# The last slab of a gated-linear-attention trunk finished in two parts of 256 tokens, with GpSimd scaling the first part of the result

## The reference, cut to what matters

```python
y = concat(y_h, y_g) @ w_out ;  h = h + y
e = rms_norm(p @ ple_proj, ple_norm_w)
gate = sigmoid(rms_norm(h, ple_gate_norm_w) @ ple_gate_w + ple_gate_b)
h = h + gate * e
return rms_norm(h, final_norm_w)          # row norm over all 2048 features
```

## Time and profile before

| what | us |
|---|---|
| median of three runs | 2304.66 |
| the profiled execution | 2304.73 |
| its span, first to last instruction | 2302.7 |

### The profile page before, as it was taken

How to read it: one execution, slowest core, us unless ns; L and a number is a source line. 1 busy time by engine, 2 the same in 40 slices (tenths; PEclk the granted TensorE clock), 3 DMA queues, 4 the chain that set the end, 5 groups by cost and what they waited for, 6 DMA issues and landing times.

```text
span 2302.7 us, 30712 instructions
## 1 busy us (share of the span) xinstructions
PE 2234.5 (97%) x10528; PEld 1855.6 (81%) x10528; DVE 1476.4 (64%) x2913; ACT 998.4 (43%) x1695; POOL 0.2 (0%) x4
## 2 busy tenths in 40 slices
PE   6999999999999999999999999999999999999995
PEld 5688888888888878888888888887888887787884
DVE  4667777775576567677766555566336456767776
ACT  5444455444343434444444333442224334446443
POOL 0000000000000000000000000000000000000000
PEclk9999999999999999999999999999999999999997
DMA  7522222222222224222222222223644543343452
GB/s 277 187 84 86 82 80 93 94 79 82 88 93 90 83 74 156 82 81 92 94 79 78 96 93 81 83 92 102 207 128 158 167 160 101 119 128 100 150 166 103
DMA packets 88501, 257.24 MB, mean 112 GB/s; under 512 B 9296, under 2 KB 9552, under 8 KB 88432
## 3 DMA queue, kind: packets, MB, share of 16 engines
q1 hardware_dynamic: 88432, 256.35, 33.7%
HBM read 231.15 MB, written 25.17 MB: 111 GB/s over the span
## 4 chain that ended last, share of the span: by engine, by line
PE 89%; DVE 4%; ACT 3%; DMA 2%; issue 1%; SPq 0%; DVEq 0%; ACTq 0%; POOLq 0%
PE acc L497 26%; PE acc L499 26%; PE acc L498 26%; PE lv L562 3%; PE so L551 1%; PE so L573 1%; PE so L571 1%; DMA e_scratch<-work 1%; DVE w_lo L1111 1%; DVE act_lo L1130 1%; DMA w_raw<-in_slabs 1%; ACT act_hi L770 1%; PE ms L540 1%; ACT w_hi L727 1%; PE tr L585 0%
## 5 line engine op out<-in xcount | busy, mean ns | idle before, releaser
L497 PE MATMUL acc<-act_hi,w_lo 128*128 128x512 f32 x2880 | 1158.2, 402 | 34.3 <-DMA vecs<-in_vec 12.2
L498 PE MATMUL acc<-act_lo,w_hi 128*128 128x512 f32 x2880 | 1126.8, 391 | 0.0
L499 PE MATMUL acc<-act_hi,w_hi 128*128 128x512 f32 x2880 | 1126.5, 391 | 0.0
L497 PEld LDWEIGHTS acc<-act_hi,w_lo 128*128 128x128 f32 x2880 | 544.6, 189 | 153.9 <-issue 16.0
L499 PEld LDWEIGHTS acc<-act_hi,w_hi 128*128 128x128 f32 x2880 | 543.2, 189 | 114.9
L498 PEld LDWEIGHTS acc<-act_lo,w_hi 128*128 128x128 f32 x2880 | 544.8, 189 | 104.2 <-issue 1.7
L727 ACT CAST w_hi<-w_raw 128x1024 fp32r<-128x1024 f32 x356 | 358.3, 1047 | 495.5 <-PE acc L499 444.5
L1111 DVE TENSOR_TENSOR w_lo<-w_raw,w_hi 128x1024 fp32r<-128x1024 f32 x356 | 419.7, 1219 | 80.1 <-ACT w_hi L727 79.9
L784 ACT ACTIVATE work<-work 128x512 f32<-128x512 f32 x120 | 75.7, 630 | 170.6 <-DVE work L1167 169.9
L741 ACT ACTIVATE work<-work 128x512 f32<-128x512 f32 x96 | 60.7, 633 | 129.3 <-DVE work L1147 129.3
L1181 DVE COPY_PREDICATED work<-mask_sb,lv 128x256 f32<-128x256 uint8 x168 | 88.7, 528 | 7.3
(11 more groups left out here) (212 smaller groups left out, 1808.5 us busy)
## 6 DMA issues: line engine op xcount, KB each, us to landing
w_raw<-in_slabs SPq DMA_DIRECT2D x356, 512.0 KB, 4.1
work<-e_scratch SPq DMA_DIRECT2D x64, 256.0 KB, 4.7
feat<-in_x_feat SPq DMA_DIRECT2D x8, 1024.0 KB, 11.1
e_scratch<-work SPq DMA_DIRECT2D x32, 256.0 KB, 2.2
state_h<-in_x_feat SPq DMA_DIRECT2D x32, 256.0 KB, 2.6
y_scratch<-work SPq DMA_DIRECT2D x16, 256.0 KB, 2.0
y_scratch<-work SPq DMA_DIRECT2D x8, 512.0 KB, 2.8
feat<-y_scratch SPq DMA_DIRECT2D x4, 1024.0 KB, 9.0
```

The source lines that it names most:

```text
L497: nc.tensor.matmul(ps, lhs_lo, rhs_hi, start=start, stop=False)
L498: nc.tensor.matmul(ps, lhs_hi, rhs_lo, start=False, stop=False)
L499: return nc.tensor.matmul(ps, lhs_hi, rhs_hi, start=False, stop=stop)
```

## The change

The last slab's 48 matmuls of 512 columns become twice 48 of 256 columns: first all for tokens 0 to 255 into `acc[1]`, then all for tokens 256 to 511 into `lv_ps[0]`. The gate chain of that tile is made once for each part, `last_first(0)`, `last_rest(0)`, `last_first(1)`, `last_rest(1)` on VectorE and two `g_gate` calls on ScalarE. The row sums, the variance, the inverse root and the four correcting instructions are made for each part too. When the first part's factor is done, `fr_ready` lets GpSimd scale all 16 tiles for tokens 0 to 255; VectorE scales the 16 tiles for tokens 256 to 511. SyncE stores each part with five DMAs of 4, 4, 4, 2 and 2 tiles: first the five of part 0 (waiting for GpSimd), then the five of part 1 (waiting for VectorE). The core of the diff:

```diff
+        PARTS = (slice(0, TH // 2), slice(TH // 2, TH))
-        ROWS_X, ROWS_H, ROWS_E, ROWS_F = (1, 2), (3, 6), (4, 5), (7, 8)
+        ROWS_X, ROWS_H, ROWS_E, ROWS_F = (1, 2), (3, 6), (4, 5), (7, 8, 9)
 @@ sync
-            for n in range(KT):
-                store_out(1, n)
-            sp.wait_ge(out_stored, HALVES * KT * 16)
+            STORES = (4, 4, 4, 2, 2)
+            for u in range(2):
+                n = 0
+                for count in STORES:
+                    n += count
+                    sp.wait_ge((f_part, f_scaled)[u], n + u * KT)
+                    sp.dma_start(out[1, n - count:n, :, PARTS[u]].rearrange("k p n -> p k n"),
+                                 work[:, n - count:n, PARTS[u]]).then_inc(out_stored, 16)
 @@ gpsimd
+            pool.wait_ge(fr_ready, 1)
+            for n in range(KT):
+                nc.gpsimd.tensor_tensor(work[:, n, PARTS[0]], work[:, n, PARTS[0]],
+                                        f_r[1][:, PARTS[0]], ALU.mult).then_inc(f_part, 1)
 @@ tensor
-            with pe.Fori(1, KT // 2) as i:
+            with pe.Fori(1, KT // 2 - 1) as i:
                 g_pair(1, i)
-            row_sums(ROWS_F[1], g2_ready, 2 * KT, g_sum[1])
+            slab(SLABS - 2, 0, t_of(SLABS - 2) // 2)
+            for part, cols in enumerate(PARTS):
+                ...
+                for k in range(KT):
+                    last = passes((acc[1], lv_ps[0])[part][:, cols], ..., act_hi[:, k, cols], act_lo[:, k, cols], ...)
+                last.then_inc(acc_ready, 1)
+            for part, cols in enumerate(PARTS):
+                row_sums(ROWS_F[1 + part], g2_ready, 2 * KT + part, g_sum[1], cols)
 @@ scalar
-            g_gate(1, 15)
-            row_rsqrt(ROWS_F[1], f_r[1], g_sum[1])
+            for part, cols in enumerate(PARTS):
+                g_gate(1, 15 + part, cols)
+            for part, cols in enumerate(PARTS):
+                row_rsqrt(ROWS_F[1 + part], f_r[1], g_sum[1], cols)
 @@ vector
-            for par in range(2):
-                g_tile(1, 7, par, False)
-            row_factors(ROWS_F[1], f_r[1], g_sum[1])
-            for n in range(KT):
-                f_scale(1, n)
+            g_tile(1, 7, 0, False)
+            last_first(0)
+            last_rest(0)
+            last_first(1)
+            last_rest(1)
+            row_variance(ROWS_F[1], PARTS[0])
+            row_variance(ROWS_F[2], PARTS[1])
+            row_root(ROWS_F[1], f_r[1], g_sum[1], PARTS[0]).then_inc(fr_ready, 1)
+            st.mark(row_root(ROWS_F[2], f_r[1], g_sum[1], PARTS[1]))
+            st.wait()
+            for n in range(KT):
+                f_scale(1, n, PARTS[1])
```

More of the change, by code:

```diff
@@ L224, in build @@
         x1_sq, r_x1 = r_e0[:, :], r_e0[:, :]
+        ALL = slice(0, TH)
+        PARTS = (slice(0, TH // 2), slice(TH // 2, TH))
         xt_sb = [state_h[:, 0:TH], state_h[:, TH:2 * TH]]
@@ L267, in build @@
         tr_ps, ms_ps = bank("tr"), bank("ms")
-        ROWS_X, ROWS_H, ROWS_E, ROWS_F = (1, 2), (3, 6), (4, 5), (7, 8)
-        rows_ps = {1: lv_ps[0], 2: lv_ps[1], 3: so_ps[0], 4: so_ps[1], 5: lv_ps[0], 6: lv_ps[1], 7: tr_ps, 8: ms_ps}
+        ROWS_X, ROWS_H, ROWS_E, ROWS_F = (1, 2), (3, 6), (4, 5), (7, 8, 9)
+        rows_ps = {1: lv_ps[0], 2: lv_ps[1], 3: so_ps[0], 4: so_ps[1], 5: lv_ps[0], 6: lv_ps[1], 7: tr_ps, 8: ms_ps, 9: so_ps[0]}
         const_loaded, glrw_loaded = sem("const_loaded"), sem("glrw_loaded")
@@ L317, in build @@
         f_scaled, out_stored = sem("f_scaled"), sem("out_stored")
+        f_part, fr_ready = sem("f_part"), sem("fr_ready")
         act_steps, vec_steps = sem("act_steps"), sem("vec_steps")
@@ L479, in _ @@
                         store_out(0, 2 * c - 3)
-            for n in range(KT):
-                store_out(1, n)
-            sp.wait_ge(out_stored, HALVES * KT * 16)
+            STORES = (4, 4, 4, 2, 2)
[6 more added lines that the diff above has]
+                                 work[:, n - count:n, PARTS[u]]).then_inc(out_stored, 16)
+            sp.wait_ge(out_stored, (KT + 2 * len(STORES)) * 16)
         @block.gpsimd
@@ L491, in _ @@
                 pool.sem_inc(s, credit)
+            pool.wait_ge(fr_ready, 1)
+            for n in range(KT):
+                nc.gpsimd.tensor_tensor(work[:, n, PARTS[0]], work[:, n, PARTS[0]], f_r[1][:, PARTS[0]], ALU.mult
+                                        ).then_inc(f_part, 1)
         @block.tensor
@@ L605, in glr_product, with row_sums @@
                 last.then_inc(glr_ready, 1)
-            def row_sums(no, added, count, total):
+            def row_sums(no, added, count, total, cols=ALL):
                 pe.wait_ge(added, count)
-                nc.tensor.matmul(rows_ps[no][:, :], ones[:, :], total, start=True, stop=True).then_inc(rows_ready, 1)
+                nc.tensor.matmul(rows_ps[no][:, cols], ones[:, :], total[:, cols], start=True, stop=True).then_inc(rows_ready, 1)
             def rec_hooks(R, nb):
@@ L707, in _ @@
             g_pair(1, 0, ({}, {2: lambda: row_sums(ROWS_F[0], g2_ready, KT, g_sum[0])}), fill=5)
-            with pe.Fori(1, KT // 2) as i:
+            with pe.Fori(1, KT // 2 - 1) as i:
                 g_pair(1, i)
-            row_sums(ROWS_F[1], g2_ready, 2 * KT, g_sum[1])
+            g = SLABS - 2
+            slab(g, 0, t_of(g) // 2)
+            g = SLABS - 1
+            for part, cols in enumerate(PARTS):
+                pe.wait_ge(acc_free[1], t_of(g) // 2 + 1)
+                pe.wait_ge(w_hi_ready, g * 2 + 2)
+                pe.wait_ge(w_lo_ready, g * 2 + 4)
+                for k in range(KT):
+                    wc = slice((k % 8) * P, (k % 8 + 1) * P)
+                    last = passes((acc[1], lv_ps[0])[part][:, cols], w_hi[1][:, k // 8, wc], w_lo[1][:, k // 8, wc],
+                                  act_hi[:, k, cols], act_lo[:, k, cols], k == 0, k == KT - 1)
+                last.then_inc(acc_ready, 1)
+            for part, cols in enumerate(PARTS):
+                row_sums(ROWS_F[1 + part], g2_ready, 2 * KT + part, g_sum[1], cols)
         @block.scalar
@@ L727, in split_weights, with softplus, sigmoid, row_rsqrt @@
                     nc.scalar.copy(w_hi[par][:, j, :], w_raw[j][:, :]).then_inc(w_hi_ready, 1)
-            def softplus(no, src, ready_sem, ready_val, bias=None):
+            def softplus(no, src, ready_sem, ready_val, bias=None, cols=ALL):
                 act.wait_ge(ready_sem, ready_val)
                 act.wait_ge(ls_ready, no + 1)
-                st.mark(A(t1, src, ACT.Abs) if bias is None else A(t1, src, ACT.Abs, bias=bias))
+                a = t1[:, cols]
+                st.mark(A(a, src, ACT.Abs) if bias is None else A(a, src, ACT.Abs, bias=bias))
                 st.wait()
-                st.mark(A(t1, t1, ACT.Exp, scale=-1.0))
+                st.mark(A(a, a, ACT.Exp, scale=-1.0))
                 st.wait()
-                A(t1, t1, ACT.Ln, bias=1.0).then_inc(sp_ready, 1)
-            def sigmoid(no):
+                A(a, a, ACT.Ln, bias=1.0).then_inc(sp_ready, 1)
+            def sigmoid(no, cols=ALL):
                 act.wait_ge(ls_ready, no + 2)
-                A(t2, t2, ACT.Exp).then_inc(sig_ready, 1)
-            def row_rsqrt(no, dst, tmp):
+                A(t2[:, cols], t2[:, cols], ACT.Exp).then_inc(sig_ready, 1)
+            def row_rsqrt(no, dst, tmp, cols=ALL):
                 act.wait_ge(rvar_ready, no)
-                st.mark(A(tmp, rows_ps[no][:, :], ACT.Ln))
+                st.mark(A(tmp[:, cols], rows_ps[no][:, cols], ACT.Ln))
                 st.wait()
-                A(dst, tmp, ACT.Exp, scale=-0.5).then_inc(ry0_ready, 1)
+                A(dst[:, cols], tmp[:, cols], ACT.Exp, scale=-0.5).then_inc(ry0_ready, 1)
             def fill_high(a, k):
@@ L1055, in g_split, with g_gate @@
                 split_weights(c + (s_gate(h) + 2), par)
-            def g_gate(h, c):
-                softplus(gate_sp(h, c), g_t, g_arg, c + (h * KT + 1))
-                sigmoid(gate_sp(h, c))
+            def g_gate(h, c, cols=ALL):
+                softplus(gate_sp(h, c), g_t[:, cols], g_arg, c + (h * KT + 1), cols=cols)
+                sigmoid(gate_sp(h, c), cols)
                 act.wait_ge(g2_sum, c + (h * KT + 1))
-                A(t1, g_t, ACT.Square).then_inc(g2_sq, 1)
+                A(t1[:, cols], g_t[:, cols], ACT.Square).then_inc(g2_sq, 1)
             def g_pair(h, i):
@@ L1112, in low_weights, with row_variance, row_root @@
                                     ALU.subtract).then_inc(w_lo_ready, 1)
+            def row_variance(no, cols=ALL):
+                vec_e.wait_ge(rows_ready, no)
+                v.tensor_scalar(rows_ps[no][:, cols], rows_ps[no][:, cols], 1.0 / D, EPS, ALU.mult, ALU.add).then_inc(rvar_ready, 1)
+            def row_root(no, dst, total, cols=ALL):
+                vec_e.wait_ge(ry0_ready, no)
+                return newton(dst[:, cols], dst[:, cols], rows_ps[no][:, cols], total[:, cols])
             def row_factors(no, dst, total):
```

(35 more changed lines are left out.)

## The result

The changed kernel takes 2312.3 us (median of 8 runs, 2311.41 to 2313.94) against 2305.65 us (8 runs) of the kernel before measured beside it: a ratio of 1.003, 95% interval 1.002 to 1.0041. Its profiled execution took 2312.25 us, with a span of 2310.4.

What follows compares the result with a forecast made beforehand. TensorE, busy for 97% of the span, bounds the kernel except at its end. GpSimd's scaling ends at 2302.3, plus 7.96 to the span's end gives 2310.2; plus 2.03, less 0.07, gives 2312 us, range 2305.5 to 2317.

Steps and rivals of the forecast that it cites:

- The total: Whole kernel: span 2310.2 against 2302.7, 7.5 us longer, time 2312 us; chance 0.55.
- to VectorE taking up part 0: Start of the last tile's gate work: VectorE begins part 0 at 2274.00, 0.9 us earlier than before.
- The chain in series: Gate chain of the last tile: two parts without overlap, 4.83 us each, g_sum complete at 2283.7, 1.3 us later.
- The product: Last slab on TensorE: 0.12 us per 256-column matmul, part 0 ready at 2269.9, part 1 about 2275.6, no one waiting.
- The row factor: After g_sum: part 1's row sum 1.35 us with hand-over, part 0's factor ready at 2287.2, 2.0 us earlier.
- GpSimd beside VectorE: Final scaling: engines take whole-instruction turns, 0.60 + 0.335 = 0.935 us a tile, GpSimd ending at 2302.3.
- The stores: After GpSimd's end: in-order issue leaves 2.36 MB, 6.18 us at 382 GB/s, 7.96 us to the span's end.
- A rate far from 382: Stores after GpSimd's end: a rate far from 382 GB/s would show the prediction wrong; no price taken for 1 KB pieces.
- free overlap: Final scaling: engines overlap freely, GpSimd at 0.60 us a tile, time 2306.9, 2.2 us slower; chance 0.25.
- GpSimd at over 0.75 by itself: Final scaling: engines overlap freely but GpSimd is slow; 0.9 us a tile gives 2311.6, 1.22 gives 2316.7; chance 0.11.
- The other side: Final scaling: GpSimd undisturbed near VectorE's pace, DMA engines set the end, time 2303.3, 1.4 us faster; chance 0.06.
- The weight load: Last slab's product: weight loads bind 256-column matmuls at 0.19 us, part 1's chain starts 3.2 us later, time 2315; chance 0.03.

Runs made afterwards that it cites:

- the last three kernels: Against the kernel before: product and gate chain in two interleaved parts, no GpSimd; same with one factor and whole tiles; first with TensorE kept busy: 2303.43, 2304.35, 2302.07 us.

## Why the prediction was right

**The total** was met partly by luck. From the product's start, forecast and measured:

| piece | forecast, us | measured, us |
|---|---|---|
| to VectorE taking up part 0 | 10.19 | 9.34 |
| two gate chains | 9.66 | 9.83 |
| row factor | 3.6 | 3.37 |
| GpSimd's scaling | 15.0 | 13.69 |
| from there to the span's end | 7.96 | 8.72 |
| sum | 46.4 | 44.95 |

The last slab was thus 1.4 us shorter than forecast, and it began 1.64 us later in the profiled execution than in that of the kernel before; so the span came out at 2310.4 for a forecast of 2310.2. As a difference the forecast was 7.3 us (2312 less 2304.66), and 6.65 was measured.

**The chain in series** was right: two times 4.92 us for the 4.83 of the sum, g_sum complete 9.8 us after the first part is taken up. (The 0.61 that it names for half the columns is that of the two-input multiplies, 0.42 of 0.69; its own 4.50 is 0.63 of the 7.15 before.)

**The product** was right: 0.120 us for a 256-column matmul, and nobody waited for it in the changed kernel. As soon as the chain was shorter VectorE did wait for it, 0.57, 1.70 and 0.94 us in the last three kernels.

**The row factor** was right: forecast from the complete g_sum at 2283.7 to GpSimd's start at 2287.3 is 3.6 us, measured 3.37; part 1's row sum took 1.22 us of the 1.35 with the hand-over.

**GpSimd beside VectorE** was right in its mechanism, which no row of the kernel before could show: both engines are slowed, and it happens when both read two inputs from SBUF. Its size was the first term that was off. I had 0.60 for GpSimd and 0.335 for VectorE's turn, 0.935 in all. Measured are 0.68, 0.335 and together 0.863. So GpSimd alone is dearer than taken, and the turns are not whole: 0.15 of the 1.015 us overlap. That the second is held for the other's whole instruction, as the prediction has it, is therefore not quite borne out. Sixteen of them took 13.69 us where I had 15.0, 1.3 less. The 2.6 cycles an element that the Trainium skill gives ("GPSIMD Engine Reference", "Elementwise — side-by-side cycle accounting") would make 0.555 us, as estimated there; the measured 0.715 an instruction decides.

**The stores** were right in the order's price: GpSimd's end to the span's end was forecast at 7.96 and measured 8.72. The second term that was off is the rate: I took no price for 1 KB pieces, and 2.36 MB at 342 GB/s instead of 382 are 0.72 us more, nearly all of the 0.76. A rate far from 382 was one of the prediction's own signs of being wrong; 342 is 10% off.

The rivals: free overlap is excluded by the groups with and without VectorE beside; GpSimd at over 0.75 by itself too. The other side, GpSimd at VectorE's pace, needed under 0.465 us a tile, and it has 0.68 alone: by the prediction's own sum, 16 x 0.68 without any disturbance would give a time of 2308.1, an estimate. No run has both engines at once and undisturbed; with the engines apart, VectorE held back too, it was 2309.87. The weight load does not bind at 256 columns: the matmuls stand 0.120 us apart, where the rival needed 0.19.

## What to carry to other kernels

Before a second engine is given half of an elementwise loop, ask what both read: two engines that each read two SBUF operands do the pair in 0.86 us where VectorE alone does both in 0.67. A queue that issues in order turns the slower engine's end into the time at which the faster one's results may leave, so stores should be written in the order in which results come ready. And a dependent chain over two engines that is cut in two pays only when its parts are interleaved: counted from the product's start, which takes in the early start, its end came 0.5 to 1.4 us later than uncut in series (five kernels) and 1.7 us earlier side by side (three). Taken by itself the chain was 2.3 us longer in series, and side by side 0.9 shorter where VectorE waited 0.57 us for part 1.

## What the runs showed of the hardware that was not expected

- GpSimd and VectorE do not exclude each other for whole instructions. At 256 columns the pair takes 0.863 us, where 0.68 and 0.335 alone would make 1.015; a GpSimd multiply of 256 columns adds 0.53 us to each VectorE multiply whether that has 256 or 512 columns.
- Stores in 1 KB pieces flow at 342 GB/s, in 2 KB pieces at 380 to 382, both with the DMA engines' share at 1.0.
- The same row sum over 256 columns has two prices. In the changed kernel part 0's began 2.6 us after the product, with the granted clock at 1.00 up to its start, and took 0.78 us; part 1's, 4.15 us after that one, had 0.50 and took 1.22. With VectorE waiting for GpSimd, part 0's began 3.4 us after the product, at 0.50, and took 1.22 as well.
